# Moving eight of the 31 taps of a depthwise convolution from VectorE to GpSimd

## The reference

```
ada = silu(c) @ w_ada + b_ada                  # shifts, scales, gates
u = x * (1 + sc1) + sh1
q, k, v, glu_in, g_attn, g_conv = split(u @ w_in)
attn = 8 heads of causal softmax attention, head size 64
a, g = split(glu_in)                           # 512 channels each
h = a * sigmoid(g)                             # (256, 512)
h = causal depthwise convolution of h over 31 positions + dw_b
y_conv = silu(layer_norm(h)) @ w_pw
merged = sigmoid(g_attn) * (attn @ w_attn_br) + sigmoid(g_conv) * y_conv
x = layer_norm(alpha * x + (1 + gt1) * (merged @ w_out))
... then an MLP with relu squared and a second layer norm
```

## Time and profile before

| | us |
|---|---|
| runs, median of 3 (1937.77 to 1939.8) | 1939.33 |
| the profiled execution's own time | 1941.2 |
| its span, first to last instruction | 1939.4 |
| TensorE, VectorE, ScalarE, GpSimd busy | 1808.5, 1306.2, 870.9, 53.8 |
| the taps with three operands, 232 at L916 | 102.5 |
| VectorE's weight splits in the first block, 232 at L129 | 280.6 |

### The profile page before, as it was taken

One profiled execution on the slowest core, in us unless ns is written; L12 is line 12 of the kernel. 1 busy time (PEld: TensorE's weight loads), 2 busy tenths in 40 slices (PEclk: granted clock), 3 DMA queues, 4 the chain that ended last, 5 costly groups with the idle time before them and its releaser, 6 DMA issues.

```text
span 1939.4 us, 26122 instructions
## 1 busy us (share of the span) xinstructions
PE 1808.5 (93%) x8358; PEld 1423.0 (73%) x8358; DVE 1306.2 (67%) x2015; ACT 870.9 (45%) x1458; POOL 53.8 (3%) x116
## 2 busy tenths in 40 slices
PE   7989989998989999996699999999999999999997
PEld 3755767886755678884699767788879976778886
DVE  4679886666779886555454788655555478865554
ACT  1434433443334434442355565444445566644443
POOL 0000000000000000000000000000000000000000
PEclk9999999999999999998799999999999999999999
DMA  8755567773755546652566433455565553355653
GB/s 291 250 159 169 182 206 246 243 248 104 260 160 172 174 162 233 202 195 69 187 184 191 147 104 120 152 185 184 178 207 181 178 163 123 102 160 176 195 176 117
DMA packets 210879, 345.90 MB, mean 178 GB/s; under 512 B 20105, under 2 KB 95799, under 8 KB 210533
## 3 DMA queue, kind: packets, MB, share of 16 engines
q1 hardware_dynamic: 208758, 337.79, 53.8%
q0 software_dynamic: 2032, 6.97, 1.1%
HBM read 343.62 MB, written 1.07 MB: 178 GB/s over the span
## 4 chain that ended last, share of the span: by engine, by line
issue 52%; POOLq 1%; POOL 0%; DVE 0%
POOLq L1631 0%; POOLq L1620 0%; POOLq L1629 0%; POOL x_rstd L1632 0%; DVE x_res L1856 0%; POOL gates L1614 0%; POOL x_rstd L1633 0%; POOL sub_rstd L1621 0%; POOL x_squares L1628 0%; POOLq L1639 0%; POOLq L1454 0%; POOL lat_rstd L1621 0%; POOLq L377 0%
## 5 line engine op out<-in xcount | busy, mean ns | idle before, releaser
L129 DVE TENSOR_TENSOR w_lo_b<-w_raw_b,w_hi_b 128x1024 fp32r<-128x1024 f32 (+3 forms) x336 | 362.2, 1100 | 189.5 <-ACT w_hi_b L123 187.9
L123 ACT CAST w_hi_b<-w_raw_b 128x1024 fp32r<-128x1024 f32 (+3 forms) x336 | 313.4, 951 | 167.2 <-PE prod_b L145 79.6
L129 DVE TENSOR_TENSOR w_lo_a<-w_raw_a,w_hi_a 128x1024 fp32r<-128x1024 f32 x232 | 280.6, 1222 | 136.5 <-ACT w_hi_a L123 133.8
L143 PE MATMUL prod_b<-w_hi_b,hT_hi 128*128 128x512 f32 (+1 forms) x912 | 342.7, 376 | 14.3 <-ACT proj_b L1661 8.2
L123 ACT CAST w_hi_a<-w_raw_a 128x1024 fp32r<-128x1024 f32 x232 | 240.9, 1049 | 234.2 <-PE acc_a L145 115.1
L145 PE MATMUL prod_b<-w_hi_b,hT_lo 128*128 128x512 f32 (+1 forms) x912 | 334.6, 367 | 0.0
L144 PE MATMUL prod_b<-w_lo_b,hT_hi 128*128 128x512 f32 (+1 forms) x912 | 333.5, 366 | 0.0
L143 PE MATMUL prod_a<-w_hi_a,uT_hi 128*128 128x512 f32 x592 | 244.8, 413 | 18.3 <-DVE w_lo_a L129 9.4
L145 PE MATMUL prod_a<-w_hi_a,uT_lo 128*128 128x512 f32 x592 | 237.6, 401 | 0.0
L144 PE MATMUL prod_a<-w_lo_a,uT_hi 128*128 128x512 f32 x592 | 237.5, 401 | 0.0
L143 PEld LDWEIGHTS prod_b<-w_hi_b,hT_hi 128*128 128x128 f32 x912 | 173.1, 190 | 45.7 <-DVE w_lo_b L129 13.0
(11 more groups left out here) (320 smaller groups left out, 2446.5 us busy)
## 6 DMA issues: line engine op xcount, KB each, us to landing
w_raw_a<-in_w_in_dram SPq DMA_DIRECT2D x72, 512.0 KB, 4.2
w_raw_b<-in_w_in_dram SPq DMA_DIRECT2D x192, 172.0 KB, 2.4
w_raw_a<-in_w_up_dram SPq DMA_DIRECT2D x64, 512.0 KB, 4.7
w_raw_a<-in_w_down_dram SPq DMA_DIRECT2D x64, 512.0 KB, 4.5
ada_raw<-in_w_ada_dram SPq DMA_DIRECT2D x52, 512.0 KB, 6.6
w_raw_b<-in_w_gate_dram SPq DMA_DIRECT2D x96, 256.0 KB, 3.1
w_raw_b<-in_w_ffn_gate_dram SPq DMA_DIRECT2D x88, 256.0 KB, 3.5
w_raw_b<-in_w_ffn_up_dram SPq DMA_DIRECT2D x88, 256.0 KB, 4.2
```

Of the source, the lines that this page charges most:

```text
L123: act.copy(self.hi[:, s, 0:cols], self.raw[:, s, 0:cols]).then_inc(self.hi_done, 1)
L129: dve.tensor_tensor(self.lo[:, s, 0:cols], self.raw[:, s, 0:cols], self.hi[:, s, 0:cols].bitcast(F32), ALU.subtract).then_inc(self.lo_done, 1)
L143: pe.matmul(out, a_hi, w_hi, start=first and c == 0, stop=False)
```

## The change

In each pair, VectorE computes taps 0 to 22 and GpSimd taps 23 to 30. GpSimd multiplies tap 23 into `pool_sum`, and for each of the other seven multiplies into `pool_tap` and adds that to `pool_sum`, with a drain ahead of each addition and one behind it. It starts on the same turn as VectorE, and from the second pair on also waits for the last pair's `conv_done`. VectorE keeps its four weight splits, and every split now stands four taps earlier in its order of taps (the first after tap 9, the second after tap 13 and the scores, the third after tap 17); then it sums its two accumulators, does the last split, waits for GpSimd, adds `pool_sum`, and only then signals `conv_done`.

```diff
+DVE_TAPS = 23
+        pool_sum, pool_tap = sb("pool_sum", [P, SEQ]), sb("pool_tap", [P, SEQ])
+        pool_taps_done = sem("pool_taps_done")
 (gpsimd, after the four loads)
+                for t in range(PAIRS):
+                    T.taken(pool, layer(l, F_PAIR + 4 * t, F_ALL))
+                    if l or t:
+                        pool.wait_ge(conv_done, layer(l, t, PAIRS).count(0))
+                    for k in range(DVE_TAPS, CONV_K):
+                        rows, w = hpad[:, k:k + SEQ], conv_wT[:, t, k:k + 1]
+                        pool.tensor_scalar((pool_sum if k == DVE_TAPS else pool_tap)[:, :], rows, w, None, ALU.mult)
+                        if k > DVE_TAPS:
+                            pool.drain()
+                            pool.tensor_tensor(pool_sum[:, :], pool_sum[:, :], pool_tap[:, :], ALU.add)
+                            pool.drain()
+                    pool.sem_inc(pool_taps_done, 1)
                 for tok in range(TOKS):
                     norm_rstd(layer(l, tok, TOKS).count(1), conv_mv, conv_rstd, tok)
 (vector, pair)
                     if t < PAIRS - 1:
                         gated(t + 1)
-                    taps(range(0, 14), conv_w)
+                    taps(range(0, 10), conv_w)
                     W.split_lo(dve, nxt)
-                    taps(range(14, 18), conv_w)
+                    taps(range(10, 14), conv_w)
                     for h in range(2):
                         H.lows(dve, n, h, HD ** -0.5, hide)
                     W.split_lo(dve, nxt + 1)
                     for h in range(2):
                         H.norm(dve, n, h)
-                    taps(range(18, 22), conv_w)
+                    taps(range(14, 18), conv_w)
                     W.split_lo(dve, nxt + 2)
-                    taps(range(22, CONV_K), conv_w)
+                    taps(range(18, DVE_TAPS), conv_w)
                     dve.drain()
-                    dve.tensor_tensor(conv_acc[0][:, :], conv_acc[0][:, :], conv_acc[1][:, :], ALU.add).then_inc(conv_done, 1)
+                    dve.tensor_tensor(conv_acc[0][:, :], conv_acc[0][:, :], conv_acc[1][:, :], ALU.add)
                     W.split_lo(dve, nxt + 3)
+                    dve.drain()
+                    dve.wait_ge(pool_taps_done, at(1, PAIRS, 1).count(0))
+                    dve.tensor_tensor(conv_acc[0][:, :], conv_acc[0][:, :], pool_sum[:, :], ALU.add).then_inc(conv_done, 1)
```

## The result

The changed kernel takes 1957.6 us in the median (1955.8 to 1958.0) against 1939.6 beside it: a ratio of 1.0091, interval 1.0079 to 1.0103, or 18 us slower. The forecast was slower, by 36 us.

What follows compares the result with a forecast made beforehand. It took a 24.4 us loop per pair to bound the kernel: VectorE to the probabilities, then TensorE to the next `hpad`. 1941.2 + 21 + 15 = 1977, less 1.9 for the median: 1975, range 1943 to 2008.

Steps and rivals of the forecast that it cites:

- VectorE's delay: VectorE before the probabilities: GpSimd's reads add 4.5 us a pair (3.1 to 6.1), net +2.64 us, eight times: +21 us.
- the first leg: VectorE's part of each pair, from `hpad` to the first head's probabilities: 14.4 us of the 24.4 us loop.
- six clock falls of 2.55 us: TensorE in six steady pairs: 3.6 us of idleness ahead of the probabilities lowers its clock, 2.55 us each, +15 us.
- The limit before: Pair loop of 24.4 us; TensorE's 23.4 us of work is the floor, so shortening VectorE's part gains at most 1.0 us.
- VectorE is held while GpSimd reads: SBUF reads: VectorE's two-operand instructions wait while GpSimd reads, 0.27 us a product and 0.56 an addition, 6.1 us a pair.
- The rival in which VectorE doesn't wait: SBUF reads: only GpSimd waits, its 17 us are hidden, and the kernel gains 9.7 us, to 1930; chance 0.13.
- The price of GpSimd's instructions: GpSimd's 128x256 work: 0.46 us a product, 0.75 an addition, 0.15 a drain; 11.0 us a pair alone.
- GpSimd's queue: GpSimd's loads and `norm_rstd` around the loop: its last sum is done before VectorE's statistics, no cost.
- The moved signal and the extra sum: VectorE behind the probabilities: later `then_inc` and added sum cost nothing, or 1.6 us a pair if uncovered.
- the cover: Behind the probabilities: 1.5 us between VectorE's 7.4 us and TensorE's 8.9 us to the transpose of `conv_acc`.
- The two legs: Behind the probabilities: VectorE's 7.4 us from the last normalisation's end, TensorE's 8.9 us to the transpose of `conv_acc`.
- The rival at 1960, the clock stays: TensorE's steady pairs: the idleness brings no slow clock, so only +21 us, 1960; chance 0.20.

Runs made afterwards that it cites:

- the additions kernel: Changed kernel with GpSimd doing all seven additions and only the first two products, the other six products left out: 1959.1 us, ratio 1.0099.
- the two kernels that leave parts out: Changed kernel with GpSimd's eight products and no additions: 1930.4 us; changed kernel with its seven additions and only two products: 1959.1 us.

## Why the prediction was right in kind and wrong in size

The step that failed is the size of VectorE's delay: 4.5 us a pair in the first leg, where the runs show 3.4; after the 1.86 us of taps taken out, that leaves 1.5 instead of 2.64. With it failed the term that hung on it, six clock falls of 2.55 us, where there were four of 1.2 to 2.9. The mechanism held.

- *The limit before.* Right that TensorE waits for the probabilities and that VectorE's leg is paid in full. Incomplete in two points. VectorE was also full as a whole, which the timeline showed (no gap from 141.52 to 165.95) and I read as a leg only. And taking work from VectorE for nothing would have given 16 us, not 10: the floor of a steady pair is 22.9 us, not 23.4, which is 3 us, and the first pairs gave 6.1 us, not 3.7.
- *VectorE is held while GpSimd reads.* Right, though no row showed it beforehand. The rival in which VectorE doesn't wait is refuted by the tap of 0.96 us and by the gain with GpSimd idle.
- *The price of GpSimd's instructions.* An addition at 0.75 us: 0.74 in the median of the additions kernel, 0.83 in the changed one. A product at 0.46: 0.92. Wrong by a factor of two; the row for one column said nothing about a multiplication by a per-partition scalar.
- *"VectorE's delay lies between 3.1 and 6.1; I take 4.5", all of it in the first leg.* This is the first term that was mis-sized. By the two kernels that leave parts out, the two kinds together would cost 8 x 0.14 + 7 x 0.46 = 4.3 us if all met what they met there, close to the 4.5. In the changed kernel VectorE's work in pair 1 is 24.5 us against 21.1 with GpSimd idle: 3.4, with the extra sum in both. A product and an addition follow each other every 2.0 us and not every 1.5, so in pair 1 only six products and four additions had begun when VectorE came to the scores at 154.70; of the rest some met the score and normalisation steps (one of 0.29 us took 0.52), some the taps behind the probabilities, where VectorE has time. The first leg grew by 12.1 / 8 = 1.5 us a pair instead of 2.64: 12 us instead of 21. So the delay in it was 1.5 + 1.86 = 3.4 us a pair on average, not 4.5.
- *Six clock falls of 2.55 us, 15 us.* The second term: four falls, 6.7 us. The idle time was 1.9 to 3.0 us and not 3.6. In this trace the clock stayed after 1.92 and 1.96, fell for 3.4 us after 2.25 to 2.64 (1.2 to 1.4 us lost), and for 6.8 after 3.00 (2.86 lost); the other kernels don't keep to this order. Since the second term hung on the first, one wrong size counted twice. The two first pairs lost 0.8 us less to the clock than before, which I had put at nothing.
- *GpSimd's queue.* Right: VectorE never waits for GpSimd at the new sum, and GpSimd's last addition of pair 1 ends at 161.43, 6.6 us before VectorE wants it.
- *The moved signal and the extra sum.* Right that they cost nothing in this kernel, but the cover was never 1.5 us thick. The two legs don't start together: VectorE's 7.4 us start at 156.5, TensorE's 8.9 at 155.97, so the rows gave 0.9. In pair 1 of the changed kernel 0.13 were left, and in the kernels with less delay in the first leg the cover is gone.
- *The rival at 1960, the clock stays.* It lies nearest to 1957.6, but by luck: it has 21 us of delay and no fall, and the runs show 12 and 6.

Of the 18 us, 12 are delay and 6 the clock that follows from it (6.7 less 0.8). The delay is shown by the run with GpSimd idle, the clock by the one with TensorE's idle time filled.

## What to carry to other kernels

Semaphores are not the only tie between engines. A VectorE instruction that reads two operands from SBUF and a GpSimd instruction that reads SBUF delay each other; a three-operand tap given away saved 0.465 us, and its replacement, a product and an addition beside such taps, cost 0.14 + 0.46 us on the engine it was to relieve. What cost VectorE little here was GpSimd's writing (0.32 us a pair, all on one-operand `tensor_scalar`), and what wasn't delayed by GpSimd's additions was the score step that reads PSUM and one SBUF operand (0.54 to 0.55 us beside them and alone). Read a loop from both sides, the legs and each engine's sum: where two limits coincide, an edit that moves only one of them wins little. A signal that is moved to the end of an engine's work costs nothing only while another leg is the longer one. And where a forecast holds a cost that may or may not come, such as a clock fall, sum it with the smaller delay too.

## What the runs showed of the hardware that I had not expected

GpSimd's product of 128x256 by a per-partition scalar (0.92 us) takes longer than its sum of two tensors (0.73 us), but holds VectorE for a third as long. Fifteen writes of 128x256 (0.31 us each) lengthen none of its three-operand taps, but do lengthen its one-operand `tensor_scalar`: 0.35 us alone for the second tap of a pair, 0.51 beside the writes, and 0.48 to 0.83 beside the products of the changed kernel, in seven pairs of eight. TensorE's clock fell after 1.67 and 1.90 us of idleness and stayed at 1.00 after 2.43 and 3.38.
